# One slab remainder on GpSimd as four instructions of 512 columns in place of one of 2048

## The reference, cut to what matters

```python
for l in range(DEPTH):                                      # DEPTH = 2
    x = x + 0.5 * swiglu(rms_norm(x, ffn1_norm[l]), ffn1_w_in[l], ffn1_w_out[l])
    z = rms_norm(x, mix_norm[l]) @ mix_w_in[l]              # mixer input
    ...                                                     # three mixers: fox, rwkv7, moba
    x = x + concat([y_fox, y_rwkv, y_moba]) @ mix_w_out[l]  # mixer output
    x = x + memory_cross_attention(rms_norm(x, ...), rms_norm(mem, ...), ...)
    x = x + 0.5 * swiglu(rms_norm(x, ffn2_norm[l]), ffn2_w_in[l], ffn2_w_out[l])
...                                                         # second block: attention, gated delta net
x = x + g1 * merge_branches(attn_x, gdn_x, gate_x, w_pa, w_pd, w_out)
x = x + g2 * conv_ffn(modulate(rms_norm_2(x), sh2, sc2), w_up, ffn_conv_w, ffn_conv_b, w_down)
```

## Time and profile before

| | |
|---|---|
| median of 3 runs | 2870.01 us (2865.53 to 2876.79) |
| the profiled execution | 2866.49 us, span 2864.7 us |
| busy PE / DVE / ACT / POOL | 84% / 47% / 40% / 43% of the span |
| mean granted clock of TensorE | 0.893 of full speed |
| line 363 on POOL | 242 instructions, 1120.1 us |

### The profile page before, as it was taken

The page is one execution under the profiler, slowest core; times in us unless marked ns, Lnnn a source line. Parts: engine busy times, 40 slices in busy tenths (PEclk is TensorE's granted clock), DMA queues, the critical chain, the costliest instruction groups (busy, mean ns, idle before and its releaser), DMA issues. The chain is left out here.

```text
span 2864.7 us, 42748 instructions
## 1 busy us (share of the span) xinstructions
PE 2410.8 (84%) x18099; PEld 2095.9 (73%) x18099; DVE 1348.1 (47%) x2101; ACT 1137.3 (40%) x1543; POOL 1238.2 (43%) x308
## 2 busy tenths in 40 slices
PE   5998988786998998988867899689867775987878
PEld 4997855384997998955466899567656665987877
DVE  5513663433722521755241721276746664335990
ACT  4433431344443442422343442447832332533333
POOL 3974500151975874600042786332200000765555
PEclk8999978797999999979887999899967777999989
DMA  4654411231554554501332454412000001553432
GB/s 147 201 178 127 133 45 59 96 120 35 191 172 129 196 176 119 179 30 60 103 103 74 142 182 131 135 59 74 16 1 1 1 1 45 168 170 103 147 125 96
DMA packets 298691, 305.98 MB, mean 107 GB/s; under 512 B 7249, under 2 KB 294461, under 8 KB 298493
## 3 DMA queue, kind: packets, MB, share of 16 engines
q1 hardware_dynamic: 298493, 303.16, 33.1%
HBM read 302.09 MB, written 1.05 MB: 106 GB/s over the span
## 5 line engine op out<-in xcount | busy, mean ns | idle before, releaser
L363 POOL TENSOR_TENSOR slab_lo<-ring,slab_hi 128x2048 fp32r<-128x2048 f32 (+1 forms) x242 | 1120.1, 4644 | 982.9 <-ACT slab_hi L354 863.6
L354 ACT CAST slab_hi<-ring 128x2048 fp32r<-128x2048 f32 (+1 forms) x242 | 450.9, 1867 | 568.8 <-PE bank L397 273.8
L428 PE MATMUL bank<-ffn_h_hi,slab_hi 128*128 128x256 f32 x1408 | 351.3, 286 | 5.6 <-ACT slab_hi L354 3.4
L429 PE MATMUL bank<-ffn_h_lo,slab_hi 128*128 128x256 f32 x1408 | 349.0, 285 | 0.0
L428 PEld LDWEIGHTS bank<-ffn_h_hi,slab_hi 128*128 128x128 f32 x1408 | 273.3, 194 | 10.9 <-ACT slab_hi L354 5.8
L429 PEld LDWEIGHTS bank<-ffn_h_lo,slab_hi 128*128 128x128 f32 x1408 | 273.2, 194 | 0.1
L433 PE MATMUL bank<-ffn_h_hi,slab_lo 128*128 128x256 f32 x1408 | 200.7, 286 | 20.7 <-POOL slab_lo L363 20.7
L1445 POOL TENSOR_TENSOR inv_m<-inv_d,const 128x512 f32<-128x512 f32 x24 | 30.3, 1268 | 427.0 <-ACT inv_d L1503 322.4
L433 PEld LDWEIGHTS bank<-ffn_h_hi,slab_lo 128*128 128x128 f32 x1408 | 183.4, 194 | 22.3 <-POOL slab_lo L363 22.3
L395 PE MATMUL bank<-ffn_hidden_hi,slab_hi 128*128 128x256 f32 x704 | 199.2, 283 | 0.0
L396 PE MATMUL bank<-ffn_hidden_lo,slab_hi 128*128 128x256 f32 x704 | 199.2, 283 | 0.0
(11 more groups left out here) (585 smaller groups left out, 5963.4 us busy)
## 6 DMA issues: line engine op xcount, KB each, us to landing
ring<-in_ffn_w_in SPq DMA_DIRECT2D x88, 1024.0 KB, 5.1
ring<-in_ffn_w_out SPq DMA_DIRECT2D x32, 1024.0 KB, 5.0
ring<-in_w_in SPq DMA_DIRECT2D x30, 1024.0 KB, 5.4
ring<-in_mix_w_in SPq DMA_DIRECT2D x24, 1024.0 KB, 5.5
ring<-in_w_mod SPq DMA_DIRECT2D x24, 1024.0 KB, 5.3
ring<-in_w_up SPq DMA_DIRECT2D x22, 1024.0 KB, 5.1
ring<-in_ffn_w_out SPq DMA_DIRECT2D x16, 768.0 KB, 4.4
ring<-in_mix_w_out SPq DMA_DIRECT2D x8, 1024.0 KB, 5.1
```

The costliest lines, as they stand in the source:

```text
L354: act.copy(self.hi[i % self.PLACES][:, 0:w], K.ring[n % RING][:, 0:w]).then_inc(self.hi_ready, 1)
L363: pool.tensor_tensor(self.lo[i % self.PLACES][:, 0:w], place[:, 0:w], self.hi[i % self.PLACES][:, 0:w].bitcast(F32), ALU.subtract).then_in ...
L428: pe.matmul(out, w[0][:, k, col], act[0][:, k, :], start=(k == 0), stop=False)
L429: pe.matmul(out, w[0][:, k, col], act[1][:, k, :], start=False, stop=False)
```

## The change

POOL's subtraction of a slab is issued in four parts, each over a quarter of the columns (512, or 384 of a slab of 1536). Only the last part raises `lo_ready`, so PE and SP are told at the same point of the work as before. Nothing else changes; lines below it move by three.

```diff
             pool.wait_ge(self.hi_ready, i + 1)
-            pool.tensor_tensor(self.lo[i % self.PLACES][:, 0:w], place[:, 0:w],
-                               self.hi[i % self.PLACES][:, 0:w].bitcast(F32), ALU.subtract).then_inc(self.lo_ready, 1)
+            for part in range(4):
+                c = slice(part * w // 4, (part + 1) * w // 4)
+                last = pool.tensor_tensor(self.lo[i % self.PLACES][:, c], place[:, c],
+                                          self.hi[i % self.PLACES][:, c].bitcast(F32), ALU.subtract)
+            last.then_inc(self.lo_ready, 1)
```

## The result

The changed kernel takes 2897.41 us in the median of 4 runs (2892.09 to 2900.93), beside 2871.11 us for the kernel before in the same session (4 runs, 2865.53 to 2876.79). The ratio is 1.009, 95% interval 1.0064 to 1.0116: 18 to 33 us slower. I had predicted 2859 us, at most 2875. The profiled execution has a span of 2889.2 us, 24.5 above that of before.

What follows compares the result with a forecast made beforehand. PE was busy 84%, waiting at known stages where POOL and DVE take whole-instruction turns; terms -14 - 9.5 - 4 + 9.7 + 2 + 6 + 0.4 = -9.4 gave 2857 us profiled, 2859 median, range 2842 to 2875.

Steps and rivals of the forecast that it cites:

- exclusive turns and their strict alternation: POOL and DVE hold something in turns, a whole instruction at a time; one DVE instruction gets through between two of POOL's.
- a part's own cost: Every slab: four parts at 1.23 us from start to start make 4.92 us, +0.35 us a slab.
- the mixer output: Mixer output, twice: DVE's `mix_y_lo` get turns between POOL's parts, so PE ends earlier; -7 each, -14.
- the merge stage: Merge stage: PE's 7.8 us wait for `m_x_lo` shrinks as DVE waits for shorter parts; -4, between -2.5 and -5.5.
- the waits of an FFN start: Four FFN starts: DVE's sums fall inside slab 0, +1.9, and a product into the fourth slab, +0.35 + 0.45; +9.7 in all.
- The rival in which DVE gets no turn between parts: Whole kernel: parts that follow at once keep DVE out, so nothing is gained; +16, 2886 us, chance 0.06.
- The rival in which a part costs over 1.32 us: FFN bulk: POOL becomes the bound from 1.32 us a part; at 1.40 it is +26, about 2885; chance 0.08.
- Mixer input, twice: loss. +3 each, +6.: Mixer input: three DVE turns of 256 columns go into POOL's waited-for slabs, five times a stage; +3 each, +6.
- the clock, "0 to +4, I take +2": FFN starts: PE's longer idling can leave it at the low clock level for a stretch more; +2 taken.
- conv FFN, -9.5: Conv FFN: eight parts and eight DVE instructions alternate, 1.0 us less for two slabs; -9.5, bounds -4 and -14.
- a DVE turn of 256 columns: What one such turn costs POOL, taken from a pair of slabs in the conv FFN: 0.11 us.
- Cross attention, +0.2 a layer: Cross attention of the two layers: a small loss of +0.2 us a layer, +0.4 in the sum.

Runs made afterwards that it cites:

- experiments 9 and 10: Kernel before with four parts in the mixer input alone: 9 with its last slab whole, 2892.60 us (1.0062); 10 with only its last slab in parts, 2888.42 us (1.0069).
- experiment 8: Kernel before with four parts in the four FFN stages alone, their fourth slab whole: 2882.39 us, ratio 1.0038.

## Why the prediction was wrong

**Rightly read** were the exclusive turns and their strict alternation, a part's own cost, the mixer output (-14 predicted, -12 measured), the merge stage (-4 predicted, and its stretch 2503.1 to 2600.5 is 2.9 shorter), and the waits of an FFN start (+1.9 and +0.8 predicted, 2.04 and 0.86 found in layer 0's second FFN). The rival in which DVE gets no turn between parts is refuted by `mix_y_lo` at 6.37 us; the Trainium skill's page GPSIMD Engine Reference (instruction dispatch) is not contradicted, but what I drew from it is. What I drew from its page SBUF — State Buffer (who interferes with whom) holds: the block of a DVE instruction is now one part long. The rival in which a part costs over 1.32 us is refuted too: POOL's mean in the page has DVE's turns in it. Without them, at the start of the cross attention of layer 0, the first four parts take 4.95 us (timeline of POOL):

```profile
609.23 4.95 POOL L365 TENSOR_TENSOR slab_lo<-ring,slab_hi 128x512 fp32r<-128x512 f32 x4 [18.05 <-ACT slab_hi L354]
```

**The step that failed most: "Mixer input, twice: loss. +3 each, +6."** Measured alone: +20, and in that kernel's profile the stage is 10.3 and 10.1 us longer in the two layers. In layer 0 the 10.3 are three things. The last slab's wait grew by 2.8 us: the step counted three DVE turns of 256 columns and none of the scan. I had read DVE's rows near the first waited-for slabs and took the last to be like them; its rows are the ones shown above. The other four waits grew by 3.9 us in all, where I had some 2.5, in part because a turn costs 0.20 us and not 0.11 (the third point below). The remaining 3.6 us are PE's own: the same matmuls keep it busy longer, at the low clock behind its waits (18 of them in 4 us behind the last wait, granted clock 0.50). The prediction had put the clock at the FFN starts alone and here at nothing, without a reason.

**The second: the clock, "0 to +4, I take +2".** PE's busy time rose by 14.1 us for the same matmuls, some of it by the luck of single profiles (experiments 9 and 10). In two of the four stages a pause of 1.97 us is followed by the low level where one of 1.11 was not (experiment 8). After the first wait of a stage the low level lasts longer too. Windows of PE's first 7 us behind it, of before (wait 5.82, over at 716.84) and after (7.86, over at 725.65):

```profile
716.00:720.00 4.00, 3.16 (x15) 3.16 (x16) 3.97 (x2) 0.00 (x0) 4.00 (x2) 0.53 0.47 134
720.00:724.00 4.00, 4.00 (x36) 4.00 (x35) 3.96 (x2) 0.00 (x0) 4.00 (x2) 1.00 0.44 143
```

```profile
725.00:729.00 4.00, 3.35 (x15) 3.35 (x16) 0.00 (x0) 0.00 (x0) 4.00 (x4) 0.50 0.49 154
729.00:733.00 4.00, 4.00 (x27) 4.00 (x26) 0.00 (x0) 0.00 (x0) 4.00 (x5) 0.70 0.59 179
```

In the second pair 9 matmuls fewer pass, 1.1 us. It is not the same in each stage: the 48 matmuls behind the first wait take 7.80, 8.37, 7.41 and 8.38 us in the four stages, where they took 5.86, 7.12, 7.34 and 7.77, +3.9 in all. With 1.5 us behind the fourth slab's pause in two stages the clock makes +7, and not +2. PE's waits at the starts grew by 13.2 us, less 1.0 for a sum that it no longer waits for, where I had 9.7. Measured alone, the FFN stages came to +15 (10 to 20) for +11.7.

**The third: conv FFN, -9.5,** with a mis-sized term: a DVE turn of 256 columns costs POOL 0.19 to 0.22 us and not 0.11. Eight parts with seven turns between them take 11.23 us, against 9.9 alone (twice 4.95): 0.19 a turn. In the mixer input a slab with three such turns takes 5.6 us, 0.22 a turn. I had taken the price from a single turn, as the small difference of 9.25 and 9.13 us. The period gained 0.4 and not 1.0 us; with the merge stage it is -7 for -13.5.

**Cross attention, +0.2 a layer:** +6 measured for both, cause open.

The stages measured alone sum to 15 + 20 + 6 - 12 - 7 = +22, beside +26 (18 to 33) for the whole change. So the sum of stages is a sound way, and its terms were wrong: losses of 41 us stood against gains of 19, where I had 18 against 27.5. With terms of that size a range of -28 to +5 was too narrow to rest a forecast of no loss on.

## What to carry to other kernels

When two engines take turns at a resource, cutting one's instruction into parts moves time from the other to it. Cut only where the end that is waited for belongs to the other engine, and leave whole what is waited for itself: here that turned +26 us into -15, and into -29 with eight parts in the conv FFN. List for each waited-for slab every instruction of the other engine that can get into it, the longest above all, and not only those near the first one.

## What the runs showed of the hardware

- An added POOL instruction of 512 columns that follows at once costs about 0.12 us (four of 512 columns in 4.95 us, one of 2048 in 4.5 to 4.6). At 256 columns a part lasts 0.84 us with DVE's turns in it.
- The turns are kept even for tiny work: DVE's instructions of 12 columns last 1.06 and 1.18 us beside POOL's parts, and 0.18 alone. A long instruction needs only one gap: a scan gets in with two parts as with four.
- The granted clock of a stretch without any change differed between profiled executions, by 6 to 7.5 us of time in the mixer of each layer, and equal pauses of 1.97 us were followed by either level. A profile of one execution can be lucky by as much, so two profiles are better compared stage by stage than by their spans.
